# Hand-over between the stages of a two-stack transformer kernel: VectorE and ScalarE read the two banks in swapped order, and the second tile's steps move forward

## The reference

```
def second_block(x, norm_pre, norm_post, ...):
    for l in range(DEPTH):                                   # 2 layers
        h = rms_norm(x, norm_pre[l, 0])
        x = x + 0.5 * rms_norm(swiglu_ffn(h, ...), norm_post[l, 0])
        h = rms_norm(x, norm_pre[l, 1])
        m = hybrid_mixer(h, ...)
        x = x + rms_norm(m, norm_post[l, 1])
        h = rms_norm(x, norm_pre[l, 2])
        x = x + 0.5 * rms_norm(swiglu_ffn(h, ...), norm_post[l, 2])
    return x

def swiglu_ffn(h, w_gate, w_up, w_down):                     # 1024 -> 2816 -> 1024
    return (jax.nn.silu(h @ w_gate) * (h @ w_up)) @ w_down
```

## Time and profile before

| | |
|---|---|
| median of 3 runs | 2404.79 us |
| lowest and highest | 2404.46 and 2405.9 us |
| span of the profiled execution | 2405.0 us |
| mean granted TensorE clock in it | 0.990 of full speed |
| TensorE matmul busy | 2312.8 us, 96% |
| VectorE busy | 1751.6 us, 73% |
| ScalarE busy | 1406.6 us, 58% |

### The profile page before, as it was taken

The page is one execution under the profiler, slowest core; times in us unless marked ns, Lnnn a source line. Parts: engine busy times, 40 slices in busy tenths (PEclk is TensorE's granted clock), DMA queues, the critical chain, the costliest instruction groups (busy, mean ns, idle before and its releaser), DMA issues.

```text
span 2405.0 us, 39531 instructions
## 1 busy us (share of the span) xinstructions
PE 2312.8 (96%) x11130; PEld 1891.0 (79%) x11130; DVE 1751.6 (73%) x2344; ACT 1406.6 (58%) x1892; POOL 234.6 (10%) x296
## 2 busy tenths in 40 slices
PE   9998999999998999999999999999999999999998
PEld 7777788878777788877887877788878877777887
DVE  6778888887778888887556888765565569787555
ACT  5553777774653777774446576454454456665444
POOL 0000000000000000000000791000000009800000
PEclk9999999999999999999999999999999999999999
DMA  7334899985435799995655445465555554444652
GB/s 264 125 124 148 291 342 332 343 327 164 147 105 176 272 345 334 341 340 177 186 189 175 149 141 165 159 207 187 183 186 190 183 167 151 147 158 152 216 183 96
DMA packets 277775, 497.31 MB, mean 207 GB/s; under 512 B 20512, under 2 KB 112848, under 8 KB 277632
## 3 DMA queue, kind: packets, MB, share of 16 engines
q1 hardware_dynamic: 273440, 481.60, 59.8%
q0 software_dynamic: 4192, 14.02, 1.8%
HBM read 494.50 MB, written 1.05 MB: 206 GB/s over the span
## 4 chain that ended last, share of the span: by engine, by line
PE 70%; DVE 13%; DVEq 6%; issue 5%; ACT 3%; DMA 2%; ACTq 1%; PEldq 1%; PEld 0%; SPq 0%; POOLq 0%
PE g_bank L584 14%; PE g_bank L586 13%; PE g_bank L585 13%; PE s_bank L586 8%; PE s_bank L584 8%; PE s_bank L585 8%; DVE w_lo L573 4%; DVE conv_y L2542 2%; DVEq L2536 1%; PE t_bank L1679 1%; DMA w_raw<-in_moe_w_down_dram 1%; ACT w_hi L568 1%; PE t_bank L1828 1%; DVEq L2179 1%; PE t_bank L1575 1%
## 5 line engine op out<-in xcount | busy, mean ns | idle before, releaser
L573 DVE TENSOR_TENSOR w_lo<-w_raw,w_hi 128x1024 fp32r<-128x1024 f32 x929 | 1116.1, 1232 | 371.9 <-ACT w_hi L568 346.5
L568 ACT ACTIVATE w_hi<-w_raw 128x1024 fp32r<-128x1024 f32 x929 | 966.8, 1059 | 446.0 <-PE s_bank L586 189.9
L584 PE MATMUL g_bank<-w_hi,xt_hi 128*128 128x512 f32 (+1 forms) x1152 | 462.6, 402 | 22.2 <-DVEq L636 10.7
L586 PE MATMUL g_bank<-w_hi,xt_lo 128*128 128x512 f32 (+1 forms) x1152 | 452.3, 393 | 0.0
L585 PE MATMUL g_bank<-w_lo,xt_hi 128*128 128x512 f32 (+1 forms) x1152 | 452.1, 392 | 0.0
L584 PEld LDWEIGHTS g_bank<-w_hi,xt_hi 128*128 128x128 f32 x1152 | 221.3, 192 | 75.4 <-issue 16.6
L586 PEld LDWEIGHTS g_bank<-w_hi,xt_lo 128*128 128x128 f32 x1152 | 220.5, 191 | 46.6
L585 PEld LDWEIGHTS g_bank<-w_lo,xt_hi 128*128 128x128 f32 x1152 | 221.5, 192 | 42.5
L584 PE MATMUL s_bank<-w_hi,xt_hi 128*128 128x512 f32 x640 | 252.7, 395 | 0.0
L586 PE MATMUL s_bank<-w_hi,xt_lo 128*128 128x512 f32 x640 | 249.8, 390 | 0.0
L585 PE MATMUL s_bank<-w_lo,xt_hi 128*128 128x512 f32 x640 | 249.4, 390 | 0.0
(11 more groups left out here) (338 smaller groups left out, 2719.9 us busy)
## 6 DMA issues: line engine op xcount, KB each, us to landing
w_raw<-in_w_in_dram SPq DMA_DIRECT2D x192, 512.0 KB, 4.5
w_raw<-in_moe_w_gate_dram SPq DMA_DIRECT2D x128, 512.0 KB, 5.2
w_raw<-in_moe_w_up_dram SPq DMA_DIRECT2D x128, 512.0 KB, 5.4
w_raw<-in_moe_w_down_dram SPq DMA_DIRECT2D x128, 512.0 KB, 5.4
w_raw<-in_ffn_w_gate_dram SPq DMA_DIRECT2D x176, 256.0 KB, 2.9
w_raw<-in_ffn_w_up_dram SPq DMA_DIRECT2D x176, 256.0 KB, 3.1
w_raw<-in_ffn_w_down_dram SPq DMA_DIRECT2D x88, 512.0 KB, 3.4
w_raw<-in_w_branch_dram SPq DMA_DIRECT2D x40, 512.0 KB, 4.4
```

What stands on the lines that cost most here:

```text
L568: nc.scalar.activation(half_of(w_hi, u, h), half_of(w_raw, u, h), ACT.Copy).then_inc(hi_ready, 1)
L573: nc.vector.tensor_tensor(half_of(w_lo, u, h), half_of(w_raw, u, h), half_of(w_hi, u, h).bitcast(F32), ALU.subtract).then_inc(lo_ready, 1)
L584: nc.tensor.matmul(dst, a_hi, b_hi, start=first, stop=False)
L586: return nc.tensor.matmul(dst, a_lo, b_hi, start=False, stop=last)
```

## The change

Only the second stack's hand-overs and the start of its parts change.

- **Swapped banks.** VectorE multiplies bank 1 of a tile first, as soon as TensorE is done with it, while ScalarE squares bank 0. ScalarE waits for a new semaphore, `second_scaled`, before it squares bank 1. VectorE multiplies bank 0 after ScalarE's first square.
- **Tile 1 forward on VectorE.** Tile 1's bank 1 is multiplied right after tile 0's x and pre-norm. The sums and the reciprocal of tile 1 stand between tile 0's two low parts. Bank 0 of tile 1 is multiplied after tile 1's reciprocal. The weight half 3 now is split between tile 1's two halves of x.
- **Split transposes on TensorE.** Tile 1's two transposes, which stood together after the third step of 6 products, now stand one after the third and one after the fourth step. This also holds for the first feed-forward of the second stack.

The core of the diff (the removed lines of the old loop in `hand_over` stand in the function above):

```
@@ ScalarE, hand_over
                         for nb in range(2):
+                            if nb:
+                                act.wait_ge(second_scaled, 6 * l + (2 * i + tt + 1))
                             act.activation(junk[...], g_bank[fills[tt][nb].slot(4)][:, :], ACT.Square, ...)
@@ TensorE, first_units
-                                elif half == 1 and h == 0:
-                                    xt_quads(src, t, i, 1)
+                                elif half == 1:
+                                    xt_quads(src, t, i, 1, (h,))
@@ VectorE, hand_over
+                    dve.wait_ge(out_ready, 3 * l + (i + 1))
+                    fence(dve)
+                    scaled(0, 1).then_inc(second_scaled, 1)
+                    dve.wait_ge(square_ready, 15 * l + (sq + 1))
+                    scaled(0, 0).then_inc(g_free[fills[0][0].slot(4)], 1)
+                    root_in(0)
+                    added(0, 0)
+                    added(0, 1)
+                    unit_is_used(dve, u_last)
+                    fence(dve)
+                    scaled(1, 1).then_inc(second_scaled, 1)
+                    if nxt is not None:
+                        next_lo(0, 0)
+                    root_in(1)
+                    if nxt is not None:
+                        next_lo(0, 1)
+                    if split < 3:
+                        split_lo(u_last + 1, 2)
+                    scaled(1, 0).then_inc(g_free[fills[1][0].slot(4)], 1)
+                    added(1, 0)
+                    split_lo(u_last + 1, 3)
+                    added(1, 1)
+                    dve.drain().then_inc(x_ready, 1)
+                    if nxt is not None:
+                        next_lo(1, 0)
+                        next_lo(1, 1)
+                    split_lo(u_last + 1, 4)
```

More of the change, by code:

```diff
@@ L544, in build @@
         router_t_ready, comb_ready = sem("router_t_ready"), sem("comb_ready")
+        second_scaled = sem("second_scaled")
         def half_slot(u, h):
@@ L1752, in _, with xt_quads @@
                 first, mixer, second = layer2(l, done)
-                def xt_quads(src, t, i, tt):
-                    for kq in range(2):
+                def xt_quads(src, t, i, tt, kqs=(0, 1)):
+                    for kq in kqs:
                         pe.wait_ge(normed_ready, 12 * l + (4 * i + 2 * tt + kq + 2))
@@ L2443, in hand_over, with scaled, root_in @@
                     dve.wait_ge(post_in, 48 * l + (16 * i + 16))
-                    for tt in range(TT):
-                        def scaled(nb):
-                            cols = slice(nb * 512, (nb + 1) * 512)
-                            b = fills[tt][nb].slot(4)
-                            dve.tensor_tensor(dst[:, tt, cols], g_bank[b][:, :], gains[:, 1, cols], ALU.mult).then_inc(g_free[b], 1)
-                        dve.wait_ge(square_ready, 15 * l + (sq + 2 * tt + 1))
-                        scaled(0)
+                    def scaled(tt, nb):
+                        cols = slice(nb * 512, (nb + 1) * 512)
+                        return dve.tensor_tensor(dst[:, tt, cols], g_bank[fills[tt][nb].slot(4)][:, :], gains[:, 1, cols], ALU.mult)
+                    def root_in(tt):
                         dve.wait_ge(square_ready, 15 * l + (sq + 2 * tt + 2))
@@ L2454, in hand_over @@
                                                  in1=mean_sq[:, tt, 1:2], op0=ALU.add, op1=ALU.add)
-                        dve.drain()
+                        dve.drain().then_inc(g_free[fills[tt][1].slot(4)], 1)
                         dve.reciprocal(rstd[:, tt:tt + 1], rstd[:, tt:tt + 1]).then_inc(var_ready, 1)
-                        scaled(1)
-                        dve.drain()
-                        dve.wait_ge(rstd_ready, At(8 + n + tt, (l, 11)).value(1, 1))
-                        for nb in range(2):
-                            cols = slice(nb * 512, (nb + 1) * 512)
-                            dve.scalar_tensor_tensor(out=x[:, tt, cols], in0=dst[:, tt, cols], scalar=rstd[:, tt:tt + 1], in1=x[:, tt, cols],
-                                                     op0=ALU.mult, op1=ALU.add)
-                            if nxt is None:
-                                dve.drain().then_inc(row_out, 1)
-                            else:
-                                dst_next, layer, i_next, t_next, n_xt = nxt
-                                norm_in(dst_next, layer, i_next, tt, nb)
@@ L2469, in hand_over, with added @@
-                        if tt == TT - 1:
-                            dve.drain().then_inc(x_ready, 1)
-                        if tt == 0 and split < 3:
-                            split_lo(u_last + 1, 2)
-                        if nxt is not None:
-                            dve_xt(t_next + 2 * tt, At(16 * DEPTH + n_xt + 2 * tt, (layer, XT_LAYER2)), 2, [(tt, 0), (tt, 1)], each=True)
-                        split_lo(u_last + 1, 3 + tt)
+                    def added(tt, nb):
+                        cols = slice(nb * 512, (nb + 1) * 512)
+                        if nb == 0:
+                            dve.drain()
+                            dve.wait_ge(rstd_ready, At(8 + n + tt, (l, 11)).value(1, 1))
+                        dve.scalar_tensor_tensor(out=x[:, tt, cols], in0=dst[:, tt, cols], scalar=rstd[:, tt:tt + 1], in1=x[:, tt, cols],
+                                                 op0=ALU.mult, op1=ALU.add)
+                        if nxt is None:
+                            dve.drain().then_inc(row_out, 1)
+                        else:
+                            norm_in(nxt[0], nxt[1], nxt[2], tt, nb)
@@ new lines, in next_lo @@
+                    def next_lo(tt, kq):
+                        _, layer, _, t_next, n_xt = nxt
+                        dve_xt(t_next + (2 * tt + kq), At(16 * DEPTH + n_xt + 2 * tt + kq, (layer, XT_LAYER2)), 2, [(tt, kq)], each=True)
+                    dve.wait_ge(out_ready, 3 * l + (i + 1))
[3 more added lines that the diff above has]
+                    scaled(0, 0).then_inc(g_free[fills[0][0].slot(4)], 1)
```

## The result

In 22 runs each the changed kernel takes 2413.95 us (2405.94 to 2417.63) and the kernel before 2407.33 us (2404.46 to 2415.01), both medians. The ratio is 1.0019, 95% interval 1.0012 to 1.0026: 2.9 to 6.3 us slower, 4.6 in the middle. The means of the 22 runs (2412.9 and 2408.3 us) stand in that ratio; the medians lie further apart, 6.6 us. The ratio is within the 0.2% that the prediction called no change, but the loss is clear of zero. The forecast was 4.5 us slower; the changed kernel's time (2413.95 against 2409.3, range to 2411.0) was missed.

The account below looks back on a forecast made before the run. TensorE's next product was taken to bound the kernel, via tile 0's restart and the slackless hidden-tile chain. Terms 1.2 + 0.2 + 1.8 + 0.4 + 0.9 = +4.5 us on 2404.8 gave 2409.3 us, range 2404.6 to 2411.0.

Parts of the forecast that it names:

- What bounds the kernel: TensorE, busy 96% of the span: only delays to its next product count, through two chains at the hand-overs.
- The chain that showed in no wait: From ScalarE's last high part to the hidden tile, ready 0.16 us before use: delays pass to TensorE one to one.
- Swapped banks, tile 0: In HO3, VectorE's sum into x starts 0.36 us earlier; tile 0's last pre-norm ends at 1748.43.
- Swapped banks, tile 1: ScalarE's second square waits for VectorE: square and HO3 restart 0.87 us later; restart unchanged in the mixer's hand-overs.
- Tile 1 on VectorE: In HO3, VectorE's reordered list ends tile 1's second pre-norm 0.45 us later, although the first is some 0.7 us earlier.
- The clock: Half-speed stretch after a restart costs up to 1.6 us; HO3 taken at +1.2, HO1 and HO4 at +0.1 each.
- third rival: Clock falls in every hand-over for the full stretch: HO3 +1.8, HO1/HO4 +0.4, HO2/HO5 +1.05 each; 2410.9 us; chance 0.15.
- Split transposes: Tile 1's second transposes come 6 products later: HO2 and HO5 +0.9 us each, first feed-forward +0.4.
- Tail: Weight half 3 now precedes VectorE's second sum, delaying the last output transfer: +0.9 us, bounds +0.7 and +1.0.
- The sum: All hand-overs, first feed-forward and end of kernel together: +4.5 us, ends +1.9 and +6.3.
- the second's: Rival that the hidden tile absorbs the delay, leaving the end of the kernel and the clock: 2405.8 us; chance 0.13.
- Span and median differ by 0.2 us, so I add to the median: 2404.8 + 4.5: Whole-kernel level: the summed change added to the shown median of 2404.8 us, giving 2409.3 us.

Follow-up runs that it names:

- free: Changed kernel with tile 1's banks not swapped, so ScalarE squares both without waiting and VectorE multiplies bank 1 afterwards: ratio to the kernel before 0.9996.
- warm: Changed kernel with 20 constant transposes on TensorE ahead of tile 0's first product in the five hand-overs: ratio to the kernel before 1.0005.
- no_split: Changed kernel with both of tile 1's transposes together again after the third step: ratio to the kernel before 1.0014.
- hid: Changed kernel with weight halves 7 and 8 split after each feed-forward's first hidden tile, not before it: ratio to the kernel before 0.9995.
- tail: Changed kernel with weight half 3 split after the last sum into x where nothing follows: ratio to the kernel before 1.0010.
- split_only: Kernel before with only tile 1's transposes split on TensorE: ratio to the kernel before 0.9995.
- all: Changed kernel, tile 1's banks unswapped, transposes together, final weight half 3 after the last sum, weight halves 7 and 8 after the first hidden tile: ratio 0.9998.
- before_hid: Kernel before with weight halves 7 and 8 split after the first hidden tile: ratio to the kernel before 1.0003.

## Why the prediction was right and wrong

**What bounds the kernel: right.** The restart and the chain behind ScalarE's last high part were the two places. The chain that showed in no wait, with 0.16 us to spare, turned into waits of 1.19, 1.12 and 0.71 us. The other signs that were named came too: ScalarE's second square idle for 0.98 us, waits before the restart of 2.38 us in HO3 and 2.37 in HO1, the restart of HO2 and HO5 in place, a weight half between the last two sums.

**Swapped banks, tile 0: right.** The sum into x was forecast 0.36 earlier and came 0.33 earlier.

**Swapped banks, tile 1: right.** Forecast was a second square 0.87 later and a restart 0.87 later; measured 0.89 and 0.89, and free shows that the hold is the cause. HO2 and HO5 kept their restart within 0.06.

**Tile 1 on VectorE: nearly right.** The second pre-norm was forecast 0.45 later and ended 0.27 later. It didn't matter, since TensorE was slower.

**The clock: the term that was too small.** I took HO3 at +1.2 and HO1 and HO4 at +0.1 each, between a case at full and one at half speed. They got the stretch, and HO3 lost 1.89; in HO1 tile 1's first product moved from 15.89 to 16.32 us, +0.43, and in HO4 by 0.42. The third rival's numbers (1.8 and 0.4) were the better ones. The working gave the full stretch 1.6 us from products of 0.4 us, which makes 1.2 to 1.4; at half speed the trace of before has 0.43 us from one to the next (1751.25 to 1753.38 in five), and then 1.6 is right, as warm measured. The four traces with a restart at 8.3 and without the constant transposes (changed, no_split, hid, tail) have a stretch in 11 of 12 hand-overs out of a feed-forward; the six with a restart at 7.4 have it in 5 of 18. The trace of before had shown one stretch among three nearly equal gaps, and I took the middle; with 0.9 us more of idle time the case with a stretch deserved nearly all the weight. This is the second step that failed.

**Split transposes: right in size, with a second cause.** HO2 and HO5 were forecast at +0.9 and lost 1.05 and 1.00. split_only shows that the split alone is enough for that. But no_split, with the transposes together again, still loses 0.61 and 0.97 there, and all, which has tile 0's swap and VectorE's new list but neither the split nor the hold, loses 0.59 and 0.56. So the new list is a second cause, and the two losses don't add. The first feed-forward was forecast at +0.4 and lost 0.69. That mark lies between 21.9 and 24.8 us over the twelve traces, and it goes by the clock: in the 11 us from 3 us after the first transposes on it is 0.84 in nine traces, 1.00 in the two with the lowest marks and 0.69 in tail, which has the highest. The rows of the changed kernel and of split_only:

```profile
1103.13:1114.13 11.00, 10.00 (x41) 8.12 (x42) 7.52 (x14) 2.47 (x6) 1.06 (x2) 0.84 0.17 47
1101.52:1112.52 11.00, 9.88 (x46) 7.80 (x47) 7.60 (x15) 3.59 (x7) 1.06 (x2) 1.00 0.19 46
```

At 0.84 alone, the four kernels with the transposes together have 22.80 to 23.00, the three with the split and the old list 23.44 to 23.49, each after a wait of 0.35 us, and the two with the split and the shorter list 22.74 and 23.03. So some 0.4 to 0.7 us are the split's, with the forecast at the low end.

**Tail: right.** +0.9 forecast, +0.86 measured.

**The sum.** By the marks of this one trace: 1.89 + 2 x 0.43 + 1.05 + 1.00 + 0.69 + 0.86 = +6.4 us, against +4.5 forecast; 0.7 + 2 x 0.33 = 1.4 of the 1.9 us in between are the hand-overs out of a feed-forward, where the clock was mis-sized. The runs say +4.6 (2.9 to 6.3), so the forecast of the difference was right, and its sense too. That it came within 0.1 us is luck: two of its terms are known to be too small. In the working, the third rival's terms make 2410.8 and not 2410.9, the second's 2405.9 and not 2405.8; neither matters.

**The step that failed first is "Span and median differ by 0.2 us, so I add to the median: 2404.8 + 4.5".** The three runs shown lay at the low end of what this kernel does: 22 runs have a median of 2407.3 and reach 2415.0. And the span isn't a run's time: the profiled execution of the changed kernel took 1.6 us more than its span (2415.18 against 2413.6), as all listed runs did (1.5 to 2.0). By that the span of 2405.0 stood for about 2406.6, 1.8 above the shown median; I read the two as nearly equal, and didn't see that the median of three was low. That is 2.5 of the 4.6 us by which 2409.3 missed. From 2407.3 the same sum gives 2411.8, still 2.1 us under 2413.95, since the medians moved by 6.6 us and the sum had 4.5. The clock, put at +1.2 and twice +0.1 where the trace has +1.89 and twice +0.43, is 1.4 of that; the rest is small beside the spread of the runs. The range, 2404.6 to 2411.0, held only what the change might do and nothing for the level.

**Where the spread comes from** is open. In the changed kernel's 22 runs the time goes with the mean clock (correlation -0.87), in the 35, 35 and 21 runs of the kernel before beside the experiments it doesn't (0.07, -0.10 and 0.16), and the other kernels lie between (-0.11 to -0.77). The traces show one place: from HO1's first square to HO2's, which is mostly the mixer, it takes 259.1 to 265.6 us over the traces, with the mixer's code the same in all. The groups of TensorE's waits in that stretch of before_hid (265.6 us; columns: what was waited for, sum, times, longest) have

```profile
PE t_bank L1920 <- ACTq L1334: 4.3, 2, 2.4
PE t_bank L1979 <- ACTq L1385: 1.8, 1, 1.8
PE t_bank L1944 <- DVEq L2545: 1.2, 1, 1.2
PE t_bank L1979 <- ACTq L1370: 0.8, 1, 0.8
```

where those of before (262.0 us) have

```profile
PE t_bank L1920 <- ACTq L1334: 2.7, 2, 2.3
PE t_bank L1979 <- ACTq L1370: 0.8, 1, 0.8
```

That is 1.6 us more in one wait and two new ones of 1.8 and 1.2 us, the first two for ScalarE and the third for VectorE, all in the mixer; the rest differs little. What makes these late there in one execution and not in another was not tried.

## What to carry to other kernels

Before moving work on one engine, list what stands behind it on the engine that will wait, and look past the next product: a chain that just meets its deadline shows no wait in the profile, and its slack is the number that prices a delay. A reordering that saves waits at one place is worth having only with the list behind it made shorter, as here: the split transposes alone give nothing measurable, with two weight halves moved they give 0.17%. And a forecast of a time needs the level as much as the difference: three runs don't give it to 0.2%.

## What the runs showed of the hardware

In the hand-overs out of a feed-forward, 0.9 us of extra idle time before a burst of products made the low clock nearly certain: with about 3.3 us from the last product of one part to the first of the next, with two sets of transposes in between, 5 of 18 restarts were followed by a stretch at half speed; with the restart 0.9 us later it was 11 of 12. The time without products is not all of it: HO2 and HO5 have about the same 3.3 us, but with one idle stretch of 2.4 us in it instead of two of 0.7 and 1.2, and of their 20 restarts without constant transposes 14 had the half speed. Filling the gap with 20 transposes of a constant removed it in 10 of 10 restarts and was worth up to 1.6 us at one place. The Trainium skill ("TensorE: Matmul & The Clock Gate", section on HAM oscillation) says that idle gaps between groups of products send TensorE back to the half clock. These traces agree, and add that the same gap is followed by the half clock in one execution and not in another: behind HO3's restart at 8.33 us the clock is 0.84 in the changed kernel and 1.00 in hid, whose code is the same up to there but for the order of two weight halves early in each feed-forward.
